# Layer norms of a hybrid decoder step: scaling in tile pairs, the affine part on ScalarE, and a few sums asked for at other places

## What is computed

```
def layer_norm(x, g, b):
    xf = x.astype(jnp.float32)
    mu = jnp.mean(xf, -1, keepdims=True)
    xc = xf - mu
    var = jnp.mean(xc * xc, -1, keepdims=True)
    return (xc * lax.rsqrt(var + LN_EPS) * g + b).astype(x.dtype)
...
    h, k_new, v_new, wkv_T = token_mixer(x, ...)
    x1 = layer_norm(ALPHA * x + h, ln1_g, ln1_b)
    f, conv_T = conv_ffn(x1, ...)
    y = layer_norm(ALPHA * x1 + f, ln2_g, ln2_b)
```

## Time and profile before

| what | value |
|---|---|
| median of three runs | 873.22 us (870.77, 873.22, 873.72) |
| the profiled execution, with its launch | 872.92 us |
| its span on the core | 871.1 us |
| mean granted TensorE clock | 0.984 |
| busy: TensorE, VectorE, ScalarE, GpSimd | 815.2, 494.8, 330.9, 274.0 us |

### The profile page before, as it was taken

One profiled execution on the slowest core, in us unless ns is written; L12 is line 12 of the kernel. 1 busy time (PEld: TensorE's weight loads), 2 busy tenths in 40 slices (PEclk: granted clock), 3 DMA queues, 4 the chain that ended last, 5 costly groups with the idle time before them and its releaser, 6 DMA issues.

```text
span 871.1 us, 23141 instructions
## 1 busy us (share of the span) xinstructions
PE 815.2 (94%) x10012; PEld 763.6 (88%) x10012; DVE 494.8 (57%) x764; ACT 330.9 (38%) x569; POOL 274.0 (31%) x121
## 2 busy tenths in 40 slices
PE   6999999999887777899998999999999999999994
PEld 6899889898677676688888999999999999999994
DVE  5588766786577666265354777766667661000037
ACT  5644565454313122433265434333333331111124
POOL 0000000000297670325252444444344434344300
PEclk9999999999999999999998999999999999999997
DMA  7232133152243343703111333223322332333202
GB/s 267 84 97 74 49 98 98 49 198 61 88 116 107 107 126 118 237 15 104 58 54 44 98 113 106 80 91 98 97 86 85 98 88 89 92 88 89 85 2 99
DMA packets 32470, 83.47 MB, mean 96 GB/s; under 512 B 5144, under 2 KB 10456, under 8 KB 31728
## 3 DMA queue, kind: packets, MB, share of 16 engines
q1 hardware_dynamic: 32368, 81.98, 30.7%
HBM read 75.87 MB, written 5.91 MB: 94 GB/s over the span
## 4 chain that ended last, share of the span: by engine, by line
PE 86%; DVE 7%; ACT 3%; issue 2%; POOL 1%; DMA 0%; DVEq 0%; ACTq 0%; POOLq 0%
PE banks L1850 83%; PE banks L1904 1%; DVE z L1241 1%; DVE xx L1241 1%; PE banks L2253 1%; DVE ms L1241 1%; DVE rw L1241 1%; DVE z L1244 1%; POOL wr_lo L697 1%; DVE ssa L1505 1%; ACT x_hi L1149 0%; ACT z L1152 0%; ACT z L1212 0%; DMA w_raw<-in_w 0%; ACT nv L982 0%
## 5 line engine op out<-in xcount | busy, mean ns | idle before, releaser
L1850 PE MATMUL banks<-x_hi,w_hi 128*128 128x264 f32 (+1 forms) x784 | 207.7, 298 | 11.4 <-DVE x_lo L1241 8.9
L1850 PE MATMUL banks<-x_hi,w_lo 128*128 128x264 f32 (+1 forms) x784 | 198.3, 286 | 0.0
L1850 PE MATMUL banks<-x_lo,w_hi 128*128 128x264 f32 (+1 forms) x784 | 198.3, 286 | 0.0
L1850 PEld LDWEIGHTS banks<-x_hi,w_hi 128*128 128x128 f32 x784 | 138.9, 191 | 24.5 <-issue 11.3
L1850 PEld LDWEIGHTS banks<-x_lo,w_hi 128*128 128x128 f32 x784 | 139.1, 192 | 0.1
L1850 PEld LDWEIGHTS banks<-x_hi,w_lo 128*128 128x128 f32 x784 | 138.9, 191 | 0.0
L697 POOL TENSOR_TENSOR w_lo<-w_raw,w_hi 128x1024 fp32r<-128x1024 f32 (+1 forms) x38 | 90.6, 2385 | 152.2 <-ACT w_hi L825 152.0
L697 POOL TENSOR_TENSOR wx_lo<-w_raw,wx_hi 128x1024 fp32r<-128x1024 f32 (+1 forms) x34 | 81.8, 2406 | 100.5 <-ACT wx_hi L825 100.1
L1244 DVE SCALAR_TENSOR_TENSOR z<-z,banks 128x260 f32<-128x260 f32 (+1 forms) x24 | 12.4, 515 | 122.1 <-PE banks L1850 121.9
L1850 PE MATMUL banks<-x_hi,wx_lo 128*128 128x260 f32 x352 | 73.5, 283 | 0.0
L1850 PE MATMUL banks<-x_hi,wx_hi 128*128 128x260 f32 x352 | 73.5, 282 | 0.0
(11 more groups left out here) (254 smaller groups left out, 1713.0 us busy)
## 6 DMA issues: line engine op xcount, KB each, us to landing
w_raw<-in_w SPq DMA_DIRECT2D x87, 512.0 KB, 3.6
w_raw<-in_w SPq DMA_DIRECT2D x16, 448.0 KB, 3.3
kv<-in_ck SPq DMA_DIRECT2D x16, 192.0 KB, 4.1
kv<-in_cv SPq DMA_DIRECT2D x16, 192.0 KB, 3.4
att<-in_x SPq DMA_DIRECT2D x8, 264.0 KB, 6.0
att_out<-att SPq DMA_DIRECT2D x1, 2112.0 KB, 8.9
z<-in_xc SPq DMA_DIRECT2D x2, 1040.0 KB, 6.7
y_out<-z SPq DMA_DIRECT2D x8, 260.0 KB, 2.2
```

What stands on the lines that cost most here:

```text
L1850: return pe.matmul(out, l, r, start=start, stop=stop)
```

## The change

1. `ln_scale` and `l2_scale` on VectorE now multiply a pair of tiles by the spread reciprocal alone, in the form of the centring; the gain is no longer in it.
2. ScalarE applies gain and bias together, with a scale column and a bias column. In norm 1 `ln_high` writes `x1_hi` for all eight tiles, and `ln_shift` rewrites `z` for tiles 0, 1, 4, 5 alone. Tiles 2, 3, 6, 7 of `z` are rewritten by VectorE (`odd_shift`), once ScalarE has rounded them; GpSimd's `odd_low` waits for that through a new semaphore, `ln_zv`.
3. In `ffn_half(1, 0)` TensorE issues the sums of squares behind blocks 1 and 4, no longer 2 and 5, and in `ffn_half(2, 0)` the spread behind block 0, no longer 2.
4. In norm 2 ScalarE first takes a root of one element, then the squares; the square of the last tile's half 1 comes ahead of all eight shifts of half 0, no longer behind five. VectorE adds the last tile's half 1 after two pair scales, takes the statistics of half 1, and then does the other two pair scales.
5. Three semaphores are merged into others: the two zeroing counts into `zeroed`, `gate_landed` into `sel_landed`, `own_landed` into `bsel_landed`.

The diff, cut to its core:

```diff
@@ gpsimd @@
         def odd_low(half, i):
             pool.wait_ge(ln_hi, KT * half + 2 * i + 2)
-            pool.wait_ge(ln_z, KT * half + 2 * i + 2)
+            pool.wait_ge(ln_zv, 2 * half + i // 2 + 1)
@@ scalar @@
+        def ln_high(half, c):
+
+            ac.wait_ge(ln_n, KT // 2 * half + c // 2 + 1)
+            ac.activation(x1_hi[:, c, span(half)], z[:, c, span(half)], ACT.Identity, scale=col(C_L1G + c),
+                          bias=col(C_L1B + c)).then_inc(ln_hi, 1)
+            own(ln_hi)
+
         def ln_shift(half, c):
 
-            ac.wait_ge(ln_n, KT * half + c + 1)
-            ac.activation(x1_hi[:, c, span(half)], z[:, c, span(half)], ACT.Identity, bias=col(C_L1B + c))\
-                .then_inc(ln_hi, 1)
-            own(ln_hi)
-            ac.activation(z[:, c, span(half)], z[:, c, span(half)], ACT.Identity, bias=col(C_L1B + c)).then_inc(ln_z, 1)
+            ac.activation(z[:, c, span(half)], z[:, c, span(half)], ACT.Identity, scale=col(C_L1G + c),
+                          bias=col(C_L1B + c)).then_inc(ln_z, 1)
             own(ln_z)
...
             for c in range(KT):
-                ln_shift(half, c)
+                ln_high(half, c)
+                if c // 2 % 2 == 0:
+                    ln_shift(half, c)
...
+        ac.activation(lst[:, 4, 0:1], col(C_EPS), ACT.Sqrt)
         for c in range(KT - 1):
             l2_square(c)
         l2_last(0)
         l2_root(0)
-        for c in range(5):
-            l2_shift(0, c)
         l2_last(1)
-        for c in range(5, KT):
+        for c in range(KT):
             l2_shift(0, c)
         l2_root(1)
@@ vector @@
-        def ln_scale(half, c):
+        def ln_scale(half, i):
 
             ve.wait_ge(n_spread, SP_L + half + 1)
-            stt(z[:, c, span(half)], z[:, c, span(half)], col(C_L1G + c), banks[:, 5, 0:TH], ALU.mult, ALU.mult)\
-                .then_inc(ln_n, 1)
+            x = z[:, 2 * i:2 * i + 2, span(half)]
+            tt(x, x, across(5), ALU.mult).then_inc(ln_n, 1)
             own(ln_n)
 
+        def odd_shift(half, i):
+
+            ve.wait_ge(ln_hi, KT * half + 2 * i + 2)
+            for c in (2 * i, 2 * i + 1):
+                ins = ve.tensor_scalar(z[:, c, span(half)], z[:, c, span(half)], col(C_L1G + c), col(C_L1B + c),
+                                       ALU.mult, ALU.add)
+            ins.then_inc(ln_zv, 1)
+            own(ln_zv)
...
         ln_recip(1)
-        for c in range(KT):
-            ln_scale(1, c)
-            if c == 4:
-                even_low(1, 0)
+        ln_scale(1, 0)
+        ln_scale(1, 1)
+        ln_scale(1, 2)
+        even_low(1, 0)
+        odd_shift(1, 1)
+        ln_scale(1, 3)
         even_low(1, 2)
+        odd_shift(1, 3)
...
         for i in range(KT // 2):
             l2_centre(0, i)
-        for c in range(5):
-            l2_scale(0, c)
+        l2_scale(0, 0)
+        l2_scale(0, 1)
         l2_last(1)
-        for c in range(5, KT):
-            l2_scale(0, c)
         l2_stats(1)
+        l2_scale(0, 2)
+        l2_scale(0, 3)
         l2_centre(1, 0)
         l2_recip(1)
         for i in range(1, KT // 2):
             l2_centre(1, i)
-        for c in range(KT):
-            l2_scale(1, c)
+        for i in range(KT // 2):
+            l2_scale(1, i)
@@ tensor @@
-            if k in (2, 5):
-                ln_var(1, 2 * (k // 5))
-                ln_var(1, 2 * (k // 5) + 1)
+            if k in (1, 4):
+                ln_var(1, 2 * (k // 4))
+                ln_var(1, 2 * (k // 4) + 1)
...
-            if k == 2:
+            if k == 0:
                 ln_spread(1)
```

More of the change, by code:

```diff
@@ L340, in layer @@
     rw_ready = sem("rw_ready")
-    pre_zero = sem("pre_zero")
+    zeroed = sem("zeroed")
     v_tok_ps = sem("v_tok_ps")
@@ L453, in layer @@
     ln_z = sem("ln_z")
+    ln_zv = sem("ln_zv")
     ln_lo_even = sem("ln_lo_even")
@@ L684, in _ @@
             for c in range(0, KT, 2):
-                sp.wait_ge(ln_z, 2 * KT + KT * half + c + 2)
+                sp.wait_ge(ln_z, KT + KT * half + c + 2)
                 sp.dma_start(a["y_out"][:, c:c + 2, span(half)], z[:, c:c + 2, span(half)]).then_inc(outs, 16)
@@ L699, in w_low @@
             own(w_late_ready)
-        pool.memset(pre[:, :, 0:1], 0.0).then_inc(pre_zero, 1)
-        own(pre_zero)
+        pool.memset(pre[:, :, 0:1], 0.0).then_inc(zeroed, 1)
+        own(zeroed)
         pool.wait_ge(slot_used, N_IN)
         for r in range(NKV):
-            pool.memset(kv[96:P, r * NSB * AW:(r + 1) * NSB * AW], 0.0).then_inc(kv_zero, 1)
-            own(kv_zero)
+            pool.memset(kv[96:P, r * NSB * AW:(r + 1) * NSB * AW], 0.0).then_inc(zeroed, 1)
+            own(zeroed)
         def products(b):
@@ L1209, in l2_shift @@
         def l2_shift(half, c):
-            ac.wait_ge(ln_n, 2 * KT + KT * half + c + 1)
-            ac.activation(z[:, c, span(half)], z[:, c, span(half)], ACT.Identity, bias=col(C_L2B + c)).then_inc(ln_z, 1)
+            ac.wait_ge(ln_n, KT + KT // 2 * half + c // 2 + 1)
+            ac.activation(z[:, c, span(half)], z[:, c, span(half)], ACT.Identity, scale=col(C_L2G + c),
+                          bias=col(C_L2B + c)).then_inc(ln_z, 1)
             own(ln_z)
+        ac.activation(lst[:, 4, 0:1], col(C_EPS), ACT.Sqrt)
         for c in range(KT - 1):
@@ L1683, in ln_recip @@
             own(n_inv)
-        def ln_scale(half, c):
+        def ln_scale(half, i):
             ve.wait_ge(n_spread, SP_L + half + 1)
-            stt(z[:, c, span(half)], z[:, c, span(half)], col(C_L1G + c), banks[:, 5, 0:TH], ALU.mult, ALU.mult)\
-                .then_inc(ln_n, 1)
+            x = z[:, 2 * i:2 * i + 2, span(half)]
+            tt(x, x, across(5), ALU.mult).then_inc(ln_n, 1)
             own(ln_n)
+        def odd_shift(half, i):
[5 more added lines that the diff above has]
+            own(ln_zv)
         def even_low(half, i):
             ve.wait_ge(ln_hi, KT * half + 2 * i + 2)
-            ve.wait_ge(ln_z, KT * half + 2 * i + 2)
+            ve.wait_ge(ln_z, KT // 2 * half + i + 2)
             x = slice(2 * i, 2 * i + 2)
@@ L1714, in _ @@
         ln_scale(0, 0)
+        rwkv_sum(1, 3)
         ln_scale(0, 1)
-        rwkv_sum(1, 3)
+        rwkv_sum(1, 4)
         ln_scale(0, 2)
-        rwkv_sum(1, 4)
+        odd_shift(0, 1)
+        rwkv_sum(1, 5)
         ln_scale(0, 3)
[L1720 to L1723, removed]
+        even_low(0, 0)
         rwkv_sum(1, 6)
-        ln_scale(0, 7)
-        even_low(0, 0)
+        odd_shift(0, 3)
         rwkv_sum(1, 7)
@@ L1819, in l2_recip, with l2_scale @@
             own(n_inv)
-        def l2_scale(half, c):
+        def l2_scale(half, i):
             ve.wait_ge(n_spread, SP_M + half + 1)
-            stt(z[:, c, span(half)], z[:, c, span(half)], col(C_L2G + c), banks[:, (5, 7)[half], 0:TH],
-                ALU.mult, ALU.mult).then_inc(ln_n, 1)
+            x = z[:, 2 * i:2 * i + 2, span(half)]
+            tt(x, x, across((5, 7)[half]), ALU.mult).then_inc(ln_n, 1)
             own(ln_n)
```

21 lines of the change are left out of this document (9 added, 12 removed).

## The result

The changed kernel is slower. Its median is 876.08 us over 9 runs (873.42 to 879.83), the kernel before beside it has 871.08 us over 9 runs (870.50 to 874.81), and the ratio is 1.0051 with an interval of 1.0030 to 1.0071. The median lies inside the range given ahead, between the forecast's 874.4 and its upper end of 876.8, but the kernel is slower by more than 0.3%, a case that had been given 0.17. The kernel before was itself 2.1 us quicker here than the median from which the forecast counted (873.22), so by difference the miss is larger: 5.0 us between the medians, or 4.4 by the ratio, where the forecast had 1.2 to 1.5.

A forecast was written before the change was run, and what follows sets the result against it. TensorE was taken to bound the kernel, with norm changes felt only in its waits and the tail. From 872.92 us, norm 1 (-0.43), clock (-0.25) and tail (+2.22) gave 874.46, said as 874.4; range 871.0 to 876.8.

The forecast's parts named there:

- What bounds the kernel, and where norm 1 waits: TensorE holds 86% of the chain; layer norm changes pay only where it waits in norm 1 and after its last matmul.
- Merged semaphores and table load, 0: Joint semaphore counts are long full and the dummy root loads ScalarE's table in idle time: price 0.
- The two prices: A ScalarE operation with scale and bias columns takes 0.605 us; a tile shift on VectorE takes 0.41 us.
- rival 2: ScalarE's scale column is free, so TensorE resumes 1.55 us sooner in norm 1; 871.9 or 870.1 us in all; chance 0.08.
- Norm 1, second half, 0.43 sooner: Earlier spread and 12 ScalarE operations instead of 16 let TensorE resume at 473.08 and not 473.51 us.
- rival 4: The moves do nothing in norm 1: VectorE's two shifts take 0.55 each, restart at 473.5, 874.9 us in all; chance 0.1.
- Norm 1, first half, price 0, bound 0.2: VectorE's last mixer sum moves up to 0.4 us later, just before TensorE's column sums ask for it; no cost.
- The clock, 0.25 sooner: After norm 1's wait TensorE's clock falls again, for 3.4 us, losing 1.7 us against 1.95 before.
- rival 1: TensorE's clock stays at its upper level after norm 1's wait; 872.8 us in all; chance 0.25.
- Rival 3: The whole 6.8 us low-clock stretch lies behind TensorE's restart in norm 1; 876.2 us in all; chance 0.12.
- The tail, 2.2 later: Norm 2 after the last matmul: root 1 path 1.27 later, pair scale 0.21, eight dearer shifts 0.75.
- The sum: The profiled execution's 872.92 us less 0.43 and 0.25 plus 2.22 gives 874.46, said as 874.4 us.

The follow-up runs named there:

- e2_norm2_only: The kernel before with only norm 2 changed as in the change; 875.88 us, ratio 1.0037 to the kernel before.
- e3_gpsimd_waits: The changed kernel, with GpSimd waiting for VectorE's low part of tiles 4 and 5 before its weight subtraction; 872.98 us, ratio 1.0010 to the kernel before.
- e7_no_gain_column: The changed kernel with the gain of norm 2 left out, so its ScalarE shifts have a bias column alone; 872.4 us in one timed run.
- e4_root_early: The changed kernel, with ScalarE taking norm 2's root of half 1 after two of half 0's eight shifts; 874.28 us, ratio 1.0026 to the kernel before.
- e5_even_low_early: The changed kernel, with VectorE's low part of tiles 4 and 5 (half 0) ahead of its shift of tiles 6 and 7; 872.53 us, ratio 1.0012.
- e1_norm1_only: The changed kernel with norm 2 as in the kernel before; 874.06 us, ratio 1.0031 to the kernel before.
- e6_both: The changed kernel with the edits of `e4_root_early` and `e5_even_low_early`; 869.28 us, ratio 0.9974 to the kernel before.
- e8_before_collides: The kernel before with one added wait: VectorE's low part of tiles 4 and 5 (half 0) starts after GpSimd's second low part; 875.11 us, ratio 1.0058.

## Why the prediction was right or wrong

**What bounds the kernel, and where norm 1 waits**: right. TensorE's waits on GpSimd's low parts and the tail are where the change was felt, besides one place more.

**Merged semaphores and table load, 0**: nothing in any trace speaks against it. The load stands at 829.16 us, in idle time, and root 0 follows its statistics; `e2_norm2_only` has the load without the merged semaphores and nothing new but its tail. Neither was run alone.

**The two prices**: right (0.605 and 0.41), so rival 2 is out; the run without the column shows the shift at 0.54 with its handover again.

**Norm 1, second half, 0.43 sooner**: right, once the collision is out of the way. From the spread of the mean to the restart `e3_gpsimd_waits` took 18.95 us, against 19.41 before: 0.46 sooner. The early places of the sums gave 0.42 of it, for which the prediction had 0.5; rival 4 is out. The restart is behind `x_lo` of GpSimd, itself released by VectorE's shift, as said. The shift in the trace after, then GpSimd's row:

```profile
474.78 0.74 DVE L1700 TENSOR_SCALAR z<-z,par 128x260 f32<-128x260 f32 x2 [0.56 <-ACT x_hi L1147]
```

```profile
475.69 1.28 POOL L765 TENSOR_TENSOR x_lo<-z,x_hi 128x520 fp32r<-128x520 f32 x1 [2.54 <-DVE z L1700]
```

**Norm 1, first half, price 0, bound 0.2**: this is the step that failed. "In the first half the same moves push VectorE's last mixer sum by up to 0.4 us to 451.5, just before TensorE's column sums ask for it" looked only at when VectorE would be done. In that it was right: the last mixer sum ends 0.28 us later, and VectorE's mean starts no later (11.88 us behind the spread of half 0's reciprocal, 11.89 before). It did not follow GpSimd, whose low part moves up by VectorE's earlier shift just as it does in the second half, and whose next operation was then set against VectorE's. (That it is this shift which releases it is read from its row, `z` of L1700 where `z` of ScalarE stood; no run changed that release alone.) The cost measured is 1.9 us of idle (2.35 against 0.45), and a stretch at the lower level behind it, in four of the five traces that have the collision. The fifth, `e7_no_gain_column`, kept its clock there and so prices that stretch: from the spread of half 1's mean to the restart it took 18.99 us, where the three others with norm 1 as changed took 20.18 to 20.25, so 1.2 to 1.3 us more. Together that is 3.2 us; by the timed runs, removing the collision gives 0.41% (`e3_gpsimd_waits`), 3.6 us. Both ends of the bound were worked out from waits; none from what a VectorE operation costs beside GpSimd. That was to be read from the page of before, in the group of the feed-forward net's low parts:

```profile
L1241 DVE TENSOR_TENSOR h_lo<-hh,h_hi 128x520 fp32r<-128x520 f32 x22 | 51.6, 2348 | 23.7 <-ACT h_hi L1186 23.7
```

This is the very operation that takes 0.70 us as `x_lo` in the quiet, with a mean of 2.35 over 22 (2.07 to 2.37). One of them in the timelines of VectorE and GpSimd before:

```profile
505.43 2.37 DVE L1241 TENSOR_TENSOR h_lo<-hh,h_hi 128x520 fp32r<-128x520 f32 x1 [1.08 <-ACT h_hi L1186]
```

```profile
504.80 2.44 POOL L697 TENSOR_TENSOR w_lo<-w_raw,w_hi 128x1024 fp32r<-128x1024 f32 x1 [4.89 <-ACT w_hi L825]
```

There TensorE has other work, so it costs nothing. In norm 1 one block of TensorE hangs on it.

**The clock, 0.25 sooner**: the length of the low stretch was right, the level a toss-up. With the same two idles of 0.90 and 1.76 us, the mean over 466 to 484 us was 0.91 in the trace after (18 x 0.09 x 2 = 3.2 us at the lower level, 3.4 forecast), in `e4_root_early`, `e5_even_low_early` and `e7_no_gain_column`, and 1.00 in `e1_norm1_only`, `e3_gpsimd_waits` and `e6_both`. Windows of after, then of `e3_gpsimd_waits` (the third number from the end is the clock):

```profile
456.00:460.00 4.00, 3.69 (x19) 3.70 (x20) 1.56 (x3) 0.56 (x1) 2.51 (x1) 0.60 0.59 147
466.00:484.00 18.00, 15.25 (x110) 14.62 (x110) 10.25 (x17) 8.93 (x14) 5.00 (x3) 0.91 0.03 2
```

```profile
456.00:460.00 4.00, 4.00 (x73) 3.67 (x73) 1.19 (x2) 1.59 (x3) 1.15 (x1) 1.00 0.70 239
466.00:484.00 18.00, 15.26 (x123) 14.64 (x122) 9.48 (x14) 10.15 (x15) 7.18 (x4) 1.00 0.10 30
```

From the restart to the last matmul the four took 380.87 to 381.30 us and the three 379.36 to 379.78, so the fall costs 1.5 us (1.7 forecast). The stretch was 0.66 shorter in after than in the trace before, not 0.25; two traces with norm 1 of the kernel before differ by 0.32 in it. So rival 1 came true in some executions of one and the same timing of waits, and with three traces of seven 0.25 looks low for it. Rival 3 (6.8 us) did not occur with these waits.

**The tail, 2.2 later**: right, and term by term. The reciprocal is 1.28 later (1.27), the first of the last eight shifts another 0.20 (10.47 us behind the last matmul, 8.99 before; 0.21), and these shifts take 0.74 more (0.75). The runs cut the same sum another way: the gain column, which stands on the path twice, ahead of the root and at the end, is 1.47, order and pairing 0.8; the earlier root takes off 2.07 with the column in place.

**The sum.** 874.4 (the terms give 874.46) lacked one term, the collision, with the clock behind it. The forecast's three terms make +1.54; between the same events the traces have -0.46, -0.66 and +2.25, so +1.13. The collision's wait is 1.89, the clock behind it 1.30 (20.25 us against 18.95 in `e3_gpsimd_waits`), and the 0.78 ahead of norm 1 is scatter. That makes the 5.10 us between the two profiled executions. The median fell inside the range, but in part by luck: the range reached to 876.8 for a clock stretch that did not occur (rival 3), and the kernel before was quicker than the one that the forecast counted from.

## What to carry to other kernels

When a change lets an engine start earlier, follow what that engine does next, not only the engine that waited for it: a GpSimd operation on SBUF that slips just ahead of a short VectorE operation with two inputs in SBUF makes that one last longer than its own. Look on the page for one form of operation with two means (here 0.70 and 2.35 us); the slow one tells what the fast one will cost next to the wrong neighbour. And ahead of a root on which the other engine's path hangs, put the work that nobody waits for behind it.

## What the runs showed of the hardware

A VectorE subtraction with both inputs in SBUF, met by a GpSimd subtraction already under way, behaves as if it stood still, and the profile counts that as its busy time, not as idle. When GpSimd's 2.37 us had begun 0.10 us earlier (after) or 0.05 us (`e8_before_collides`), the 0.70 us operation took 2.83 and 2.85. It ends 0.56 us behind GpSimd's end in after, and so does the `h_lo` shown above. The Trainium skill (SBUF — State Buffer, SBUF: two separate sides) states that the two engines' shared port pair is an exclusive lock, which whichever starts first holds for the whole instruction, and that a VectorE operation with two SBUF inputs needs it against a GpSimd operation that reads SBUF; these traces agree. When VectorE had begun first, 0.45 us ahead (before), both paid: GpSimd's two subtractions took 5.25 us, where they took 4.91 and 4.90 with no such neighbour (`e3_gpsimd_waits`, `e5_even_low_early`), and VectorE's took 0.93 and not 0.70. The second is more than that rule says; no run here shows why.

TensorE's granted clock is not fixed by the order of the code: the same idles of 0.90 and 1.76 us left it at its upper level in three traces and lowered it in four, and in a stretch that the change had not touched (416 to 424 us) it fell in after (0.79) and not in before (1.00), and fell in `e8_before_collides` too (0.79), which is the kernel before up to there. Such a stretch of 3.2 us costs some 1.5 us, more than twice the 0.68 us that this change was to gain in norm 1.
